# Token sums as columns, ranks counted from behind, and an earlier start of the last stage in a one-core decoder trunk

## The reference

```
def run_trunk(x, p, ...):
    xn = rmsnorm(h, norm1_g)
    proj = xn @ w_in + b_in                      # 2048 -> 4096
    c, r_out = conformer conv of proj, RG-LRU of proj
    h = h + concatenate([c, r_out]) @ w_out
    h = h + hier_moe(rmsnorm(h, norm2_g), ...)   # best of 4 groups, 2 of its 8 experts
    gate = sigmoid(rmsnorm(h, ple_norm_g) @ w_pg + b_pg)
    h = h + gate * (p @ w_ple)
    return rmsnorm(h, final_g)
```

## Time and profile before

| | |
|---|---|
| median of 3 runs | 1493.45 us (1491.99 to 1494.37) |
| the profiled execution | 1490.41 us, of which 1488.7 us is its span |
| busy | PE 93%, DVE 41%, ACT 15%, POOL 3% |
| chain that ended last | PE 51%, DMA 40%, DVE 3%, ACT 3% |
| experts, 453 to 666 us | 421 GB/s, DMA share 1.01 |
| mean granted clock of PE | 0.985 |

### The profile page before, as it was taken

How to read it: one execution, slowest core, us unless ns; L and a number is a source line. 1 busy time by engine, 2 the same in 40 slices (tenths; PEclk the granted TensorE clock), 3 DMA queues, 4 the chain that set the end, 5 groups by cost and what they waited for, 6 DMA issues and landing times.

```text
span 1488.7 us, 19036 instructions
## 1 busy us (share of the span) xinstructions
PE 1383.9 (93%) x7574; PEld 806.0 (54%) x7574; DVE 608.9 (41%) x1030; ACT 229.1 (15%) x369; POOL 40.8 (3%) x56
## 2 busy tenths in 40 slices
PE   8999999999989999999999999989999998997995
PEld 7888888899753333333333333333333333333995
DVE  5689645544542232232223222322232223225764
ACT  2000147533200000000000000000000000003552
POOL 0000000000000000000000000000000000000000
PEclk9999999999999999999999999999999999998998
DMA  9553342345769999999999999999999999999341
GB/s 381 218 198 125 113 122 86 142 142 198 270 241 382 422 422 422 422 422 422 422 422 422 422 422 422 422 421 422 421 422 422 422 422 421 422 422 401 143 142 59
DMA packets 72523, 486.26 MB, mean 327 GB/s; under 512 B 8416, under 2 KB 12544, under 8 KB 15120
## 3 DMA queue, kind: packets, MB, share of 16 engines
q1 hardware_dynamic: 71040, 482.98, 79.8%
q0 software_dynamic: 320, 1.59, 0.3%
q10 hardware_dynamic: 1120, 1.09, 0.2%
HBM read 481.06 MB, written 5.65 MB: 327 GB/s over the span
## 4 chain that ended last, share of the span: by engine, by line
PE 51%; DMA 40%; DVE 3%; ACT 3%; issue 2%; SPq 1%; DVEq 0%; ACTq 0%
DMA ring<-in_w_up_dram 39%; PE ps L816 14%; PE ps L625 14%; PE ps L838 5%; PE ps L688 4%; PE ps L689 4%; PE ps L690 4%; PE ps L849 2%; DVE hT L1551 1%; DMA embedding_rows<-ple_stage 1%; PE ps L634 1%; SPq L472 1%; PE ps L776 1%; PE ps L777 1%; PE ps L715 1%
## 5 line engine op out<-in xcount | busy, mean ns | idle before, releaser
L816 PE MATMUL ps<-ring,xwin 128*64 128x512 f32 x1984 | 452.6, 597 | 37.5 <-DMA ring<-in_w_up_dram 37.2
L1551 DVE TENSOR_TENSOR hT<-hT,ps 128x1056 f32<-128x1056 f32 x128 | 160.4, 1254 | 373.3 <-PE ps L849 372.3
L816 PEld LDWEIGHTS ps<-ring,xwin 128*64 128x64 f32 x1984 | 150.5, 136 | 292.7 <-issue 292.7
L838 PE MATMUL ps<-ring,hid 128*64 128x512 f32 x1024 | 233.6, 610 | 18.8 <-DVE hid L1531 18.8
L625 PE MATMUL ps<-xT,ring 128*128 128x264 f32 x1024 | 229.7, 386 | 0.0
L625 PEld LDWEIGHTS ps<-xT,ring 128*128 128x128 f32 x1024 | 194.5, 190 | 33.5 <-issue 0.3
L838 PEld LDWEIGHTS ps<-ring,hid 128*64 128x64 f32 x1024 | 74.6, 140 | 154.1 <-issue 152.7
L849 PE MATMUL ps<-S,ysb 64*128 64x264 f32 x1024 | 148.3, 408 | 1.3 <-issue 0.8
L849 PEld LDWEIGHTS ps<-S,ysb 64*128 64x128 f32 x1024 | 88.4, 186 | 110.9 <-issue 102.3
L1096 ACT ACTIVATE sgl<-ps 64x512 f32<-64x512 f32 x32 | 18.8, 588 | 575.4 <-PE ps L816 575.4
L1543 DVE COPY ysb<-ps 128x512 f32<-128x512 f32 x32 | 22.1, 691 | 181.8 <-PE ps L838 181.8
(11 more groups left out here) (271 smaller groups left out, 1021.1 us busy)
## 6 DMA issues: line engine op xcount, KB each, us to landing
ring<-in_w_gate_dram SPq DMA_DIRECT2D x128, 1024.0 KB, 23.4
ring<-in_w_up_dram SPq DMA_DIRECT2D x128, 1024.0 KB, 25.4
ring<-in_w_down_dram SPq DMA_DIRECT2D x128, 1024.0 KB, 24.1
ring<-in_w_in_dram SPq DMA_DIRECT2D x32, 1024.0 KB, 7.9
ring<-in_w_out_dram SPq DMA_DIRECT2D x16, 1024.0 KB, 4.8
ring<-in_w_pg_dram SPq DMA_DIRECT2D x16, 1024.0 KB, 5.1
hT<-in_x_dram SPq DMA_DIRECT2D x4, 528.0 KB, 5.2
pleT<-embedding_rows SPq DMA_DIRECT2D x1, 2112.0 KB, 21.5
```

What stands on the lines that cost most here:

```text
L816: mm = pe.matmul(ps[part * WIN:(part + 1) * WIN, 0, :], window(k), weights(2 * j + part)[:, kk * F:(kk + 1) * F], start=(k == 0), stop=(k ...
L838: mm = pe.matmul(ps[half * WIN:(half + 1) * WIN, 2 + b, :], hid[:, t, :], weights(8 + t)[:, q * 512:(q + 1) * 512], start=(t == 0), stop=( ...
L1551: dve.tensor_tensor(group(hT, g), group(hT, g), ps[:, bank:bank + 4, 0:TOK].rearrange("p (h k) t -> p h k t", h=2), ALU.add)\
```

## The change

It touches four places.

- **Begin:** each of 16 slices is the weight matrix of three products with one column of ones (128, 128 and 8 tokens), 48 in place of 16. The inverse roots are formed on 128 x 3 numbers and spread to rows by three products with the identity (`spread_rows`), from which DVE reads directly. One embedding product stands ahead of the spreading and two behind it (`PLE_HEAD` is 3). The constants `vecs` are loaded behind the embedding's weights.
- **Router:** DVE adds the last squares ahead of other work and no longer waits for ACT's rounding of the inverse roots before the logits. `asg` is negative and `tri` turned, so that five products in place of nine count ranks from behind; DVE needs four instructions in place of fourteen for the positions. The 0/1 matrices are made half by half, and so is `spread_scale`. Seven embedding products stand ahead of the ranks and three behind (`PLE_FIRST` 7, `PLE_FRONT` 10), with ten buffers in place of three and two large stores, issued by ACT.
- **Last stage:** three embedding products come here (`PLE_LATE`). The last expert is written out: its first `w_pg` tile is rounded by ACT and its rest taken by DVE ahead of the copies of the expert's result. All four additions stand ahead of the rests. The column sum stands behind the second product, its spreading behind the third, and four PSUM banks take turns in place of three.
- **End:** two column sums in place of the last row sum, roots and spreading as at the begin, a table load ahead of the last square, and one quarter of the scaling on POOL.

The core of the diff, in the program's order for PE, ACT and DVE:

```diff
-PLE_FIRST = 5
-PLE_FRONT = 12
-PLE_HEAD = KD - PLE_FRONT
-PLE_STAGE = 3
+PLE_HEAD = 3
+PLE_FIRST = 7
+PLE_FRONT = 10
+PLE_LATE = KD - PLE_HEAD - PLE_FRONT
...
+        def token_squares(src, first=True, last=True):
+            for c in range(3):
+                r = ROWS[c]
+                mm = pe.matmul(ps[0:r, SPREAD, SSQ + c:SSQ + c + 1], src[:, c * P:c * P + r], ones[:, 0:1],
+                               start=(first and c == 0), stop=last, skip_group_check=True)
+            if last:
+                mm.then_inc(ssq_full, 1)
+        def spread_rows(n, bank=SPREAD):
+            pe.wait_ge(rstd_ready, n)
+            for c in range(3):
+                r = ROWS[c]
+                mm = pe.matmul(ps[:, bank, c * P:c * P + r], rstd[0:r, c:c + 1].broadcast_to([r, P]), ident[0:r, 0:r],
+                               start=True, stop=True)
+            mm.then_inc(spread_full, 1)
...
-            mm = pe.matmul(ps[:, 0, 0:TOK], ones[:, :], xT[:, k, :], start=(k == 0), stop=(k == KD - 1))
-        mm.then_inc(row_full, 1)
+            token_squares(xT[:, k, :], k == 0, k == KD - 1)
+        head(0)
+        spread_rows(1)
+        for m in range(1, PLE_HEAD):
+            head(m)
...
-        for c in range(3):
-            r = ROWS[c]
-            for cc in range(c + 1):
-                rr = ROWS[cc]
-                pe.matmul(ps[0:r, 6, c * 64:c * 64 + E], ones[0:rr, 0:r] if cc < c else tri[0:r, 0:r],
-                          asg[0:rr, cc, :], start=(cc == 0), stop=(cc == c))
-        for c in range(3):
-            mm = pe.matmul(ps[:, 6, 192:192 + E], ones[0:ROWS[c], :], asg[0:ROWS[c], c, :],
-                           start=(c == 0), stop=(c == 2))
+        pe.matmul(later[:, 0:2, 0:E], tri[:, :], asg[:, 0:2, :], start=True, stop=False, skip_group_check=True)
+        pe.matmul(ps[:, 3, E:2 * E], ones[:, :], asg[:, 0, :], start=False, stop=False, skip_group_check=True)
+        pe.matmul(ps[:, 3, 0:2 * E].rearrange("p (c n) -> p c n", c=2), ones[:, :],
+                  asg[:, 1:2, :].broadcast_to([P, 2, E]), start=False, stop=False, skip_group_check=True)
+        pe.matmul(later[:, 2, 0:E], tri[0:NB, :], asg[0:NB, 2, :], start=False, stop=False, skip_group_check=True)
+        pe.matmul(ps[:, 3, 0:3 * E].rearrange("p (c n) -> p c n", c=3), ones[0:NB, :],
+                  asg[0:NB, 2:3, :].broadcast_to([NB, 3, E]), start=False, stop=True, skip_group_check=True)\
+            .then_inc(ranks_full, 1)
...
-            pe.wait_ge(rs_ready, 2)
+                if j == 0:
+                    spread_scale(half)
...
+        def place_slots(half):
+            cols = slice(half * TOK, (half + 1) * TOK)
+            for c in range(2):
+                link(dve.tensor_scalar(onehot[:, c, cols], iota[:, cols], pos[:, 0, c:c + 1], None, ALU.is_equal))
+                stt(onehot[:, c, cols], iota[:, cols], pos[:, 1, c:c + 1], onehot[:, c, cols].bitcast(F32),
+                    ALU.is_equal, ALU.add).then_inc(hot_ready, 1)
...
+        pe.wait_ge(late_loaded, 32)
+        pe.wait_ge(main["added"], 4 * (E - 1) + 4)
+        for i in range(PLE_LATE):
+            ...
+            mm.then_inc(late_full, 1)
...
-                    mm = pe.matmul(ps[:, 5, 0:TOK], ones[:, :], acc4[:, i, :], start=(i == 0), stop=(i == 3))
+                    token_squares(acc4[:, i, :], i == 0, i == 3)
+            if m == 2:
+                spread_rows(3)
...
-        with act.Fori(2, E) as e:
+        with act.Fori(2, E - 1) as e:
...
+        silu_gate(main)
+        act.wait_ge(*last_use(hi_slot(KD)))
         round_weights(KD)
+        take_results(E - 1, ysb, main)
...
             place_weights(e, kc[:, 0:1], S, main)
+            if ahead is not None:
+                rest_weights(ahead)
             take_results(e, ysb, main)
...
+        act.activation(rstd[:, 3:4], ssum[:, 3:4], ACT.Sqrt)
         finish(KD - 1)
```

More of the change, by code:

```diff
@@ L355, in build @@
     ple_taken = sem("ple_taken")
-    ple_out = [sem(f"ple_out{i}") for i in range(PLE_STAGE)]
+    first_out = sem("first_out")
+    next_out = sem("next_out")
+    late_loaded = sem("late_loaded")
+    late_full = sem("late_full")
     ple_back = sem("ple_back")
@@ L678, in _, with split_product @@
                 var(n - 26)
-        def split_product(t, n, ks, hi, rest, ready):
+        def split_product(t, bank, ks, hi, rest, ready):
             pe.wait_ge(w_lo_ready, t + 1)
-            out = ps[:, n % 3, 0:TOK]
+            out = ps[:, bank, 0:TOK]
             for i, k in enumerate(ks):
@@ L783, in gather @@
                 mm.then_inc(slots_full, 1)
-                if i == 0:
-                    spread_scale()
-        def spread_scale():
-            pe.wait_ge(ple_taken, PLE_FRONT)
-            pe.wait_ge(rstd_split, 1)
-            for half in range(2):
-                cols = slice(half * TOK, (half + 1) * TOK)
-                out = ps[:, half, 0:TOK]
-                for c in range(2):
-                    pe.matmul(out, rstd_hi[:, c:c + 1].broadcast_to([P, P]), onehot[:, c, cols], start=(c == 0), stop=False)
-                    pe.matmul(out, rstd_lo[:, c:c + 1].broadcast_to([P, P]), onehot[:, c, cols], start=False, stop=False)
-                pe.matmul(out, rstd[0:NB, 2:3].broadcast_to([NB, P]), hot_few[0:NB, cols], start=False, stop=True)\
-                    .then_inc(rs_full, 1)
-            pe.wait_ge(rs_ready, 2)
+                if j == 0:
+                    spread_scale(half)
@@ new lines, in spread_scale @@
+        def spread_scale(half):
+            if half == 0:
+                pe.wait_ge(ple_taken, PLE_FRONT)
+                pe.wait_ge(rstd_split, 1)
+            cols = slice(half * TOK, (half + 1) * TOK)
+            out = ps[:, 1, 0:TOK]
+            for c in range(2):
+                pe.matmul(out, rstd_hi[:, c:c + 1].broadcast_to([P, P]), onehot[:, c, cols], start=(c == 0), stop=False)
+                pe.matmul(out, rstd_lo[:, c:c + 1].broadcast_to([P, P]), onehot[:, c, cols], start=False, stop=False)
+            pe.matmul(out, rstd[0:NB, 2:3].broadcast_to([NB, P]), hot_few[0:NB, cols], start=False, stop=True)\
+                .then_inc(rs_full, 1)
@@ L857, in no_scatter @@
             pass
+        for n in range(CT_PLE + PLE_FIRST, CT_PG - 1):
+            dense(n, CH_IN + CH_OUT, pT, 2)
         spread_few()
+        dense(CT_PG - 1, CH_IN + CH_OUT, pT, 2)
         pe.wait_ge(hp_ready, KD)
@@ L1106, in _ @@
         act.wait_ge(main["products"], 1)
-        for i in range(PLE_STAGE):
-            act.wait_ge(ple_out[i], all_spilled(i))
         silu_gate(main)
+        keep_scale(1)
         act.wait_ge(keys_out, 48)
@@ L1159, in finish @@
             act.wait_ge(h3_ready, m + 1)
-            act.activation(hg[:, m, :], hT[:, m, :], ACT.Copy, scale=vT[:, V_FN + m:V_FN + m + 1]).then_inc(hg_ready, 1)
             if m >= 3:
@@ new lines, in _, with take_slots @@
+        place_slots(0)
+        place_slots(1)
+        def take_slots(half):
+            cols = slice(half * TOK, (half + 1) * TOK)
+            for k in range(KD):
+                i = 4 * half + k // 4
+                dve.wait_ge(slots_full, i + 1)
+                if half == 0 and k == 8:
+                    dve.wait_ge(next_out, 16)
+                if k == 0:
+                    dve.wait_ge(rs_ready, half + 1)
+                stt(xsT[:, k, cols], ps[:, gather_bank(i, k % 4), 0:TOK], g2[:, k:k + 1], rs[:, cols],
+                    ALU.mult, ALU.mult).then_inc(xs_ready, 1)
@@ L1563, in _, with expert @@
         take_results(0, ysb, main)
-        def expert(e):
+        def expert(e, ahead=None):
             for g in range(3):
```

355 lines of the change are left out of this document (187 added, 168 removed).

## The result

The changed kernel takes 1496.53 us (median, 1494.40 to 1499.91), the kernel before 1491.69 us in the same series (1487.05 to 1494.37). The ratio is 1.0037, with a 95% interval of 1.0024 to 1.0051: slower by about 0.4% (the two medians lie 4.84 us, 0.32%, apart). The profiled execution took 1496.78 us, of which its span is 1494.9 us, 6.2 us more than the span before.

The account below looks back on a forecast made before the run. The chain of waits bounds the kernel, with PE alone at the begin. Terms 12.4 - 7.3 - 0.7 - 0.4 = +4.0 us gave 1494.4 on the profiled 1490.41, so 1497.4 for the median, 0.26% slower; range 1490.5 to 1502.

Parts of the forecast that it names:

- Begin: Up to PE's first `w_in` product: column sums at the lower clock start it at 31.7 against 19.26, +12.4 us.
- the 0.71 us that I took from the router's logits: Begin: a slice's price at the higher clock, from 1.42 us for two logits slices; scaled by 332/190 to 1.24 us.
- The rival with 1.0 us a slice: Begin: only half of the longer load is felt at the lower clock; term +8.6, whole +0.2 us; chance 0.19.
- The rival by which the sums run fast: Begin: one-column products raise the clock (+4.0) or loads keep their price (+3.9); whole -4.5 us; chance 0.13.
- Router: From the logits to the first expert's `down`: first expert 8.6 us earlier, 1.35 us come back, `down` moves by -7.3 us.
- One sign of being wrong: Router: ranks that wait for embedding products, listed among the signs that would show the forecast wrong.
- the third rival: Router or last stage: the lower clock meets the seven embedding products and the late copies; +2.7 us, 1500; chance 0.15.
- What is won before `down` comes out at the end: First expert: DMA share is 0.00 ahead of `down`, so a microsecond won or lost before it is one at the end.
- Last stage: Behind the experts: second product 4.5 us earlier, column sums (2.8) and spreading (1.0) come back; -0.7 us, between -2 and +1.5.
- the delay of `ysb`: Last stage: the first `w_pg` tile's rounding and rest delay the copies that `scatter` needs by 2.6 us.
- my two terms: Last stage and end: -0.7 us and -0.4 us.
- End: Final roots and scaling: -1.2 us saved, partly lost to the table load and spreading; -0.4 us, between -1.5 and +1.

Follow-up runs that it names:

- e2: Changed kernel with five 512-column products of a constant, read by nothing, ahead of the column sums; 1495.35 us, ratio 1.0030 to the kernel before.
- e1: Changed kernel with the begin alone undone: 16 row sums, roots on the row of 264; 1482.23 us, ratio 0.9951 to the kernel before.
- e6: Kernel of e1 with two constant products in each gap ahead of the first expert and its `down`; 1482.05 us, ratio 0.9934.
- e4: Changed kernel with DVE's copy of the last expert's result ahead of the first `w_pg` tile's rest; 1492.20 us, ratio 1.0011.
- e3: Changed kernel, first expert's last two `w_down` chunks requested only after the second store of embedding rows landed; 1496.15 us, ratio 1.0036.
- e5: Kernel of e1 with 35 tiny unread products ahead of the row sums, making PE's program as long as the changed kernel's; 1485.91 us, ratio 0.9968.
- e9: Kernel of e1 with three 512-column products of a constant, read by nothing, ahead of the row sums; 1485.30 us, ratio 0.9960.
- e10_together: e9 with the edits of e6 and e4, and column sums of one slice in the last stage; 1473.53 us, ratio 0.9883.

## Why the prediction was right, and where its steps were off

The forecast was 1497.4 us, slower by 0.26%; measured were 1496.53 us and 0.37%. The sign and the reason stood: a begin dearer than what the router and the end win. But the number is right partly because errors of both signs met, as the account shows: the begin was 3.3 us cheaper than forecast, all the rest 5.5 us dearer. Nor is the near hit of 1497.4 on 1496.53 a measure of the step: I had added +4.0 to a median of 1493.45, and in the series the kernel before had 1491.69, so the medians differ by 4.84 us and the two profiled spans by 6.2.

**Begin: mechanism right, a term mis-sized.** The sums ran at the lower clock from end to end. The slice cost 1.07 us, not 1.24, and the chain behind them 5.4 us, not 6.0. What was too large is the 0.71 us that I took from the router's logits, whose slices move 36 columns: with one column moving a slice costs 0.62 us at the higher clock (e2; 2.45/4 = 0.61 in e1's last stage). The factor 332/190 = 1.75 was nearly right, e2 has 1.06/0.62 = 1.71. The rival with 1.0 us a slice (+8.6) came nearer to +9.1 than the forecast did, but not by its mechanism: of the 0.51 us by which a slice's four wide loads grow in e2 (4 x 128 ns), 0.44 are felt, not half. The rival by which the sums run fast fell, and e2 shows why: even from a high clock the one-column products let it fall. Its +4.0 was also too low for its own terms: with the 6.0 us that I had for the chain behind the sums it is +6.1.

The Trainium skill's page "TensorE: Matmul & The Clock Gate", section on LDWEIGHTS, has no clock in the price of a load. e2 differs: 190 ns at 1.00 and 318 ns at 0.50 for one shape in one run. The measurement decides.

**Router: right, with an unforeseen charge.** The first expert started 9.2 us earlier than the late begin alone would have it, against 8.6 in the prediction; the gather began at 400.86, where 392.4 and the late begin of 9.1 give 401.5. One sign of being wrong came in part: the ranks began at 396.78, when the seven embedding products ended, 0.3 us behind DVE's choice (396.47). At `down` 6.0 us were left in place of 7.3, since the clock fell at the expert's start (+1.7). With that taken away (e6), `down` starts at 436.87 against 444.04 with a begin 0.2 us later than before: -7.4. So step and size were right, and the third rival's mechanism, the lower clock, came on top. I had put it at the embedding products and the last stage; at the router it came where PE waits for DVE's last slots.

**"What is won before `down` comes out at the end": right, but not all that counts there.** e1's 9.16 us came through. I had assumed, though, that `down` and the experts behind it take what they took. I had named the 1.7 us that the lower clock costs in `down`, and that it may come elsewhere, but gave it no term; `down` came out 1.2 us longer still, and the stop at the loop's entry with the lower clock behind it (+1.1) was in no term and no rival.

**Last stage: the delay of `ysb` right, the balance not.** I forecast 2.6 us; DVE's copy came 2.7 us behind the end of `down` (1369.74 - 1367.04), against 1361.72 - 1361.68 before, and e4 won 1.8 us by undoing that alone. The second product, 36.99 us behind the last `gate_up` piece before (1384.83 - 1347.84), came after 33.21 us, 3.8 less, and after 32.18 in e1, 4.8 less; I had 4.5. The four slices took 2.45 us in e1's chain (I had 2.8). What turned -0.7 into +1.4 were two stretches of the lower clock. In e1, which had none there, last stage and end together gave 139.55 - 140.86 = -1.3, against the -1.1 of my two terms. Nor does this hang on one execution: the same last stage took 123.2 to 123.6 us up to DVE's last scaling in the four profiles without a low stretch in it (e1, e3, e5, e9), and 125.7 and 126.0 in two with two of them (the changed kernel, e6); before it was 124.4. The kernel before had the clock at 0.50 from 1369.40 to 1379.64, but this cost it nothing at the second product. Here all its engines by stretch, as above, then DVE's last addition of squares:

```profile
1362.00:1383.00 21.00, 12.13 (x79) 10.80 (x80) 19.63 (x26) 17.84 (x25) 0.00 (x0) 0.76 0.71 268
```

```profile
1381.83 1.25 DVE L1603 TENSOR_TENSOR acc<-acc,sq 128x1056 f32<-128x1056 f32 x1
```

The row sum ahead of the second product needs this addition, which ended at 1383.08, and began at 1383.13: a faster first product would have waited there.

**End: right.** -0.5 against -0.4.

## What to carry to other kernels

Price a matrix product by both of its sides: with one moving column its weight loads set the price here (0.62 us a slice at the higher clock, 1.06 at the lower), and TensorE's clock did not rise in 17.12 us of such products and fell while they ran in e2. Where PE waits a microsecond or two for another engine, look at the granted clock of what follows: four wide products of a constant in two such gaps took the low stretches away (1.77 and 1.37 us in the trace), though low stretches in the last stage took the gain back in that execution. And before a named wait is removed, ask what would arrive next; if that is as late, the wait is free.

## What the runs showed of the hardware

In these kernels the length of PE's program ahead of the loop decides whether PE stands still for about 3 us at the loop's entry: 2.98, 3.21, 2.87, 3.45 and 3.02 us in five of them, nothing in the kernel before, e1_row_begin and e6_row_busy to e10_together. 35 tiny products put in far ahead of it brought the stop back.

The Trainium skill's page "Runtime: NRT & Kernel Launch", section "Instruction fetch mechanics", says that instructions come in blocks of 16 KiB and that a branch to a block not at hand waits for its transfer. The trace agrees as far as it goes: a load of 16 KB falls at the stop. But one falls at the loop's entry without a stop as well (474.4 in e1_row_begin); which block PE waits for, no run here shows.

The lower clock behind the stop cost more than the stop. The stop alone made 0.3 us at the end of the experts (e5; e3 likewise), with the lower clock behind it 2.5 us (896.1 against 893.6; 2.6 in e2 and 4.4 in e4). The clock fell there in three of the five kernels that stopped and in none of the seven that did not.
